# A hybrid two-layer trunk on one core: mixer boundaries in another order, and the first heads' side differences on GpSimd

## What is computed

```python
for layer in range(DEPTH):
    hn = rms_norm(x, norm_mix_pre[layer])
    if layer % 2 == 0:
        m = even_mixer(hn, even_w_in[i], even_gn[i], even_w_out[i], rel_bias, pos)   # RET + MoBA
    else:
        m = odd_mixer(hn, odd_w_in[i], odd_b_forget[i], odd_w_out[i])                # FoX
    x = x + rms_norm(m, norm_mix_post[layer])
    hn = rms_norm(x, norm_ffn_pre[layer])
    x = x + rms_norm(swiglu(hn, ffn_w_in[layer], ffn_w_out[layer]), norm_ffn_post[layer])
```

## Time and profile before

| | |
|---|---|
| three runs | 1187.09, 1187.13 and 1188.12 us, median 1187.13 us |
| profiled execution | 1187.56 us, of which the span from the first to the last instruction is 1185.5 us |
| TensorE busy | 1161.1 us, 98% of the span |
| VectorE, ScalarE, GpSimd busy | 712.2, 474.4 and 508.3 us |
| mean granted clock | 0.995 |

### The profile page before, as it was taken

One profiled execution on the slowest core, in us unless ns is written; L12 is line 12 of the kernel. 1 busy time (PEld: TensorE's weight loads), 2 busy tenths in 40 slices (PEclk: granted clock), 3 DMA queues, 4 the chain that ended last, 5 costly groups with the idle time before them and its releaser, 6 DMA issues.

```text
span 1185.5 us, 14108 instructions
## 1 busy us (share of the span) xinstructions
PE 1161.1 (98%) x5386; PEld 957.4 (81%) x5386; DVE 712.2 (60%) x939; ACT 474.4 (40%) x737; POOL 508.3 (43%) x282
## 2 busy tenths in 40 slices
PE   8999999979999999999999999999999999999998
PEld 6888886778888888888888888677988888888886
DVE  3786358464565566577455845876365546656673
ACT  5211347554233222175554333665523222225642
POOL 5745541676444454300467443009744445440004
PEclk9999999989999999999999999999999999999999
DMA  7899702626887332366664243025478843235663
GB/s 273 300 329 336 242 9 72 196 89 227 310 286 274 126 104 88 97 185 194 194 269 135 93 153 104 26 71 196 150 257 287 301 175 106 88 97 151 194 195 118
DMA packets 73460, 210.40 MB, mean 177 GB/s; under 512 B 5523, under 2 KB 5779, under 8 KB 73024
## 3 DMA queue, kind: packets, MB, share of 16 engines
q1 hardware_dynamic: 69496, 196.45, 49.7%
q10 hardware_dynamic: 3912, 13.27, 3.3%
HBM read 176.12 MB, written 34.89 MB: 178 GB/s over the span
## 4 chain that ended last, share of the span: by engine, by line
PE 73%; DVE 2%; ACT 1%; DMA 1%; issue 1%; POOL 1%; DVEq 0%; POOLq 0%; ACTq 0%
PE ps L1455 24%; PE ps L1457 24%; PE ps L1456 24%; DMA w_raw<-weights 1%; PE ps L1748 1%; PE ps L1713 1%; PE ps L1494 0%; POOL w_lo L442 0%; DVE x L976 0%; PE ps L1731 0%; DVE h_lo L997 0%; DVE ps L1112 0%; DVE work L1123 0%; DVE gate_x L991 0%; ACT h_hi L690 0%
## 5 line engine op out<-in xcount | busy, mean ns | idle before, releaser
L442 POOL TENSOR_TENSOR w_lo<-w_raw,w_hi 128x1024 fp32r<-128x1024 f32 (+1 forms) x191 | 463.3, 2437 | 624.7 <-ACT w_hi L567 623.0
L1455 PE MATMUL ps<-h_hi,w_hi 128*128 128x512 f32 (+1 forms) x1008 | 385.4, 382 | 7.5 <-DVE h_lo L997 7.5
L567 ACT ACTIVATE w_hi<-w_raw 128x1024 fp32r<-128x1024 f32 x252 | 257.1, 1032 | 328.1 <-DMA w_raw<-weights 210.5
L1457 PE MATMUL ps<-h_hi,w_lo 128*128 128x512 f32 (+1 forms) x1008 | 383.8, 381 | 0.0
L1456 PE MATMUL ps<-h_lo,w_hi 128*128 128x512 f32 (+1 forms) x1008 | 383.7, 381 | 0.0
L1455 PEld LDWEIGHTS ps<-h_hi,w_hi 128*128 128x128 f32 x1008 | 191.5, 190 | 43.7 <-DVE h_lo L997 8.0
L1456 PEld LDWEIGHTS ps<-h_lo,w_hi 128*128 128x128 f32 x1008 | 191.4, 190 | 35.7 <-issue 0.2
L1457 PEld LDWEIGHTS ps<-h_hi,w_lo 128*128 128x128 f32 x1008 | 191.4, 190 | 35.5
L1156 DVE TENSOR_TENSOR prod<-work,ps 128x512 f32<-128x512 f32 x44 | 30.3, 688 | 192.7 <-ACT work L755 192.7
L1457 PE MATMUL ps<-w_hi,prod_r 128*128 128x512 f32 x308 | 119.8, 389 | 0.0
L755 ACT ACTIVATE work<-ps 128x512 f32<-128x512 f32 x44 | 26.3, 598 | 219.7 <-PE ps L1457 219.7
(11 more groups left out here) (171 smaller groups left out, 1386.7 us busy)
## 6 DMA issues: line engine op xcount, KB each, us to landing
w_raw<-weights SPq DMA_DIRECT2D x140, 512.0 KB, 3.4
stage<-fold_w SPq DMA_DIRECT2D x22, 1024.0 KB, 8.3
fold_t<-stage SPq DMA_DIRECT2D x22, 1024.0 KB, 5.4
w_raw<-fold_t SPq DMA_DIRECT2D x40, 512.0 KB, 4.2
w_raw<-fold_w SPq DMA_DIRECT2D x30, 512.0 KB, 4.1
stage<-fold_o SPq DMA_DIRECT2D x8, 1024.0 KB, 8.0
fold_ot<-stage SPq DMA_DIRECT2D x8, 1024.0 KB, 5.2
w_raw<-fold_ot SPq DMA_DIRECT2D x16, 512.0 KB, 3.9
```

Of the source, the lines that this page charges most:

```text
L442: nc.gpsimd.tensor_tensor(w_lo[:, c % RING, 0:n], w_raw[:, c % RING, 0:n], w_hi[:, c % RING, 0:n].bitcast(F32), ALU.subtract).then_inc(lo_ ...
L567: nc.scalar.activation(w_hi[:, c % RING, 0:n], w_raw[:, c % RING, 0:n], ACT.Copy).then_inc(hi_done, 1)
L1455: mm(to, held[0], moved[0], start=start, stop=False, skip_group_check=more)
L1457: return mm(to, held[1], moved[0], start=False, stop=stop, skip_group_check=more)
```

## The change

Seven parts, all in the order of work; every sum is still formed.

1. The difference S3 of the heads in places 0 to 3 and its low part go from VectorE to GpSimd (`third_sides`), which reads the SBUF copies. In layer 0 this stands before `low(OUT0 + 3)`, in layer 1 before `low(OUT1 + 6)`. New semaphores carry it.
2. The high and low parts of the sides of places 4 and 5 get steps of their own in the attention tables; those of 6 and 7 stand at the start of `project_out`.
3. ScalarE makes the high parts of four output-weight chunks in layer 0 and two more in layer 1 within the attention steps.
4. TensorE does product 4 by rows, tile 0 of both chunks first, and VectorE merges and scales this tile at once; the rest of VectorE's boundary moves into `project_out` in a new order.
5. GpSimd's order in the boundaries 1 and 3.
6. ScalarE's order there.
7. `turn(b, 2)` moves from before the second half chunk to before the third.

The diff, cut to what the text speaks of (semaphores, the waits that change with them, the side operations of ScalarE and VectorE and VectorE's step tables are left out):

```diff
...
                 c0 = AFTER[b]
                 if b in (1, 3):
                     half_eps(b, 0, 2)
-                else:
-                    half_eps(b)
+                    post_rstds(b, 0)
+                    low(c0)
+                    post_rstds(b, 1)
+                    pre_rstds(b, 0)
+                    pre_rstds(b, 1)
+                    low(c0 + 1)
+                    half_eps(b, 2, 4)
+                    post_rstds(b, 2)
+                    post_rstds(b, 3)
+                    low(c0 + 2)
+                    pre_rstds(b, 2)
+                    pre_rstds(b, 3)
+                    low(c0 + 3)
+                    return
+                half_eps(b)
                 post_rstds(b, 0)
                 post_rstds(b, 1)
                 if b < 4:
                     low(c0)
                     pre_rstds(b, 0)
                     pre_rstds(b, 1)
-                    if b in (1, 3):
-                        half_eps(b, 2, 4)
                     low(c0 + 1)
                 for t in (2, 3):
                     post_rstds(b, t)
                     if b < 4:
                         low(c0 + t)
                         pre_rstds(b, t)
...
+
+            def third_sides(layer):
+
+                raw, side, held = head_raw[layer], side_raw[layer][S3_], side_r[layer][S3_]
+
+                def side_low(k):
+                    pool.wait_ge(third_hi, KH * layer + k + 1)
+                    nc.gpsimd.tensor_tensor(held[:, k, 1, :], side[:, k, 1, :], held[:, k, 0, :].bitcast(F32),
+                                            ALU.subtract).then_inc(third_ready, 1)
+                for k in range(KH):
+                    pool.wait_ge(raw_copied, KH * layer + k + 1)
+                    nc.gpsimd.tensor_tensor(side[:, k, 1, :], raw[:, k, 2 * P:SEQ], raw[:, k, 0:2 * P],
+                                            ALU.subtract).then_inc(third_summed, 1)
+                    if k:
+                        side_low(k - 1)
+                side_low(KH - 1)
 
             own(nc.gpsimd.memset(minus_half[:], -0.5))
             pre_rstds(0, 0)
@@ -537,13 +565,16 @@
                 y = ret_y_rows[:, h, :].rearrange("p (t d) -> p t d", d=HEAD)
                 pool.wait_ge(ret_normed, h + 1)
                 nc.gpsimd.tensor_tensor(y, y, ret_gate[:, :, h * HEAD:(h + 1) * HEAD], ALU.mult).then_inc(ret_y, 1)
+            third_sides(0)
             lows(OUT0 + 3, FIN0)
             boundary(1)
             lows(FIN0 + AHEAD, FOUT0)
             lows(FOUT0, FOUT0 + 6)
             lows(FOUT0 + 36, V1)
             boundary(2)
-            lows(V1 + AHEAD, FIN1)
+            lows(V1 + AHEAD, OUT1 + 6)
+            third_sides(1)
+            lows(OUT1 + 6, FIN1)
             boundary(3)
             lows(FIN1 + AHEAD, FOUT1)
             lows(FOUT1, FOUT1 + 6)
...
                 if b in (1, 2, 3):
                     c0 = AFTER[b]
                     sums(0, True, False)
+                    if b != 2:
+                        high(c0)
                     sums(1, True, False)
-                    high(c0)
+                    if b == 2:
+                        high(c0)
                     sums(0, False, True)
                     sums(1, False, True)
-                    if b in (1, 3):
-                        half_squares(b, (2, 3))
                     high(c0 + 1)
                     turned_high(b, 0)
-                    sums(2, True, False)
-                    high(c0 + 2)
-                    turned_high(b, 1)
-                    sums(2, False, True)
-                    sums(3, True, False)
-                    high(c0 + 3)
-                    sums(3, False, True)
+                    if b != 2:
+                        half_squares(b, (2, 3))
+                        turned_high(b, 1)
+                        sums(2, True, False)
+                        high(c0 + 2)
+                        sums(3, True, False)
+                        high(c0 + 3)
+                        sums(2, False, True)
+                        sums(3, False, True)
+                    else:
+                        sums(2, True, False)
+                        high(c0 + 2)
+                        turned_high(b, 1)
+                        sums(2, False, True)
+                        sums(3, True, False)
+                        high(c0 + 3)
+                        sums(3, False, True)
                     turned_high(b, 2)
                     turned_high(b, 3)
                     if b == 1:
...
                 5: lambda: head_high(RET_PLACE[1]), 6: lambda: copy_moba_v(3),
-                11: lambda: head_high(RET_PLACE[2]), 15: lambda: head_high(RET_PLACE[3]), 17: load_gains})
-            project_out(0, OUT0, OUT0 + 4)
+                11: lambda: head_high(RET_PLACE[2]), 15: lambda: head_high(RET_PLACE[3]), 17: load_gains,
+                8: lambda: high(OUT0 + 4), 13: lambda: high(OUT0 + 5), 18: lambda: high(OUT0 + 6), 20: lambda: high(OUT0 + 7),
+                16: lambda: side_highs(KH), 19: lambda: side_highs(KH + 1)})
+            project_out(0, OUT0, OUT0 + 8)
             boundary(1)
             ffn(0)
...
 
-            attention(FOX, TILES * MOBA, FOX_PLACE, FOX_BANKS, {5: lambda: high(OUT1 + 5)})
+            attention(FOX, TILES * MOBA, FOX_PLACE, FOX_BANKS, {
+                5: lambda: high(OUT1 + 5), 14: lambda: high(OUT1 + 6), 24: lambda: high(OUT1 + 7),
+                30: lambda: side_highs(KT + KH), 34: lambda: side_highs(KT + KH + 1)})
             act.dma_start(gain_pre[:], norms[3, 0].partition_broadcast(P)).then_inc(gain_pre_landed, 16)
...
                     vec.wait_ge(raw_copied, KH * (hd // KT) + hd % KT + 1)
                 nc.vector.tensor_tensor(h_lo[:, hd % KT, :], ps[:, 5 + 2 * (hd % 2), :],
                                         h_hi[:, hd % KT, :].bitcast(F32), ALU.subtract).then_inc(head_ready, 1)
-                head_sums(hd)
-                if hd % KT:
-                    side_lows(hd - 1)
+                if hd % KT >= KH:
+                    head_sums(hd)
 
             def head_sums(hd):
 
                 layer, place, k = hd // KT, hd % KT, hd % KH
                 bank, raw, n = ps[:, 5 + 2 * (hd % 2), :], head_raw[hd // KT], sums_of_heads(hd)
                 s3, s1, s2, s4 = (s[:, k, 1, :] for s in side_raw[layer])
-                if place < KH:
-                    nc.vector.tensor_tensor(s3, bank[:, 2 * P:SEQ], raw[:, k, 0:2 * P], ALU.subtract).then_inc(head_summed, 1)
-                    return
+                if place == KH:
+                    vec.wait_ge(raw_copied, KH * (layer + 1))
                 if hd == KH:
...
                     vec.wait_ge(merged, seen + 2 + t + 1)
                     merge(ps[:, 1 + 2 * t, :], 5 + 2 * t, work[:, 2 + t, :])
                 half_scale(b, (0, 1))
-                for t in range(2):
-                    vec.wait_ge(chunk_used, c0 + 10)
-                    merge(ps[:, 2 * t, :], 2 * t, work[:, t, :])
-                post(b, 0)
+                vec.wait_ge(first_row, layer + 1)
+                merge(ps[:, 0, :], 0, work[:, 0, :])
+                post_scale(b, 0)
+                vec.wait_ge(chunk_used, c0 + 10)
+                merge(ps[:, 2, :], 2, work[:, 1, :])
+                post_add(b, 0)
                 post(b, 1)
+                pre(b, 0)
                 for t in range(2):
                     vec.wait_ge(chunk_used, c0 + 12)
                     merge(ps[:, 5 + 2 * t, :], 5 + 2 * t, work[:, t, :])
+                pre(b, 1)
+                turned_low(b, 0)
+                half_scale(b, (2, 3))
+                turned_low(b, 1)
+                post(b, 2)
+                post(b, 3)
+                pre(b, 2)
+                pre(b, 3)
+                turned_low(b, 2)
+                turned_low(b, 3)
 
             def attention(heads, unit0, places, banks, table, also={}):
...
                 pe.wait_ge(h_ready, 4 * b + 2)
                 n = AHEAD - 1 if b else AHEAD
                 for i in range(n):
-                    if i == (1 if b else AHEAD - 1):
+                    if i == (n - 1 if b else AHEAD - 1):
                         turn(b, 2)
                     if i == n - 1:
...
@@ -1591,11 +1656,15 @@
                 product(1)
                 pe.wait_ge(probs, end)
                 product(2)
-                pe.wait_ge(head_summed, 16 * (layer + 1))
+                pe.wait_ge(head_summed, 3 * KH * (layer + 1))
                 pe.wait_ge(head_ready, KT * (layer + 1))
                 product(3)
                 pe.wait_ge(merged, seen + 4)
-                product(4)
+                for i in range(2):
+                    last = out_part(layer, 4, i, (0,))
+                last.then_inc(first_row, 1)
+                for i in range(2):
+                    out_part(layer, 4, i, (1,)).then_inc(chunk_used, 1)
                 pe.wait_ge(merged, seen + 6)
                 product(5)
                 pe.wait_ge(first_copied, 4 * layer + 2)
...
```

(23 more changed lines are left out.)

33 lines of the change are left out of this document (18 added, 15 removed).

## The result

Fourteen runs of the changed kernel gave 1192.59 us in the median (1187.1 to 1195.49), fourteen of the kernel before 1187.46 (1186.24 to 1188.56). The ratio is 1.004, 95% interval 1.0028 to 1.0052. The forecast was 1190.0 us. The profiled execution of the changed kernel took 1193.1 us, 5.5 more than that of before.

A forecast was written before the change was run, and what follows sets the result against it. TensorE, busy 98% of the span, was taken as the bound. From 1187.56 us, −0.5 and +3.75 (boundaries), −0.4 (FoX) and 0 (MoBA) gave 1190.4, or 1190.0 on the median; range 1180.5 to 1193.5.

The forecast's parts named there:

- Step 1: Both boundaries, first transposed tiles: they come about 0.7 us earlier, so TensorE's wait becomes 2.6 us.
- Step 3: Both boundaries, pre(2): GpSimd's low part ahead of rstd_pre(2) delays it; TensorE waits 0.4 to 0.6 us.
- Step 4: Both boundaries, pre(3): GpSimd's low part goes first and blocks it; turn(b, 3) waits 3.1 us, bounds 0.5 and 3.1.
- rival A: Boundaries, pre(3): VectorE goes first and the low part is stretched instead; 1181.4 us, chance 0.25.
- Step 5: Both boundaries, low clock after TensorE's waits: 0.5 us for the wait of 2.6, 1.9 for that of 3.1.
- FoX: FoX heads: VectorE's relief gives −2.3 us, a low part blocking s2 of head 4 costs 2.0; net −0.4, bounds −2.4, +1.5.
- rival B: Head stretches: the locks make a product wait 2 to 3 us and bring low clock; 1193.4 us, chance 0.17.
- MoBA: MoBA heads: VectorE's relief of 1.2 to 2 us against s2 blocked up to 2; taken as 0, bounds −2, +3.

The follow-up runs named there:

- the second experiment: Changed kernel, but GpSimd's low parts of output weights in the head stretches wait for VectorE's subtraction s2 of a head; 1193.04 us.
- the first experiment: Changed kernel, but in both boundaries GpSimd starts the fourth weight chunk's low part only after the last pre, pre(3); 1185.92 us.

## Why the prediction was right, and which terms were mis-sized

The side and the mechanism were right: slower, by the lock of the two engines at `pre(3)` and `s2`. Step by step:

- **Step 1** (first wait 2.6): 2.44 in both boundaries. Right.
- **Step 3** (`pre(2)` 5.0 us after TensorE's start): 838.00 − 833.02 = 4.98. Right. TensorE did not wait for it: it was at half clock and came later.
- **Step 4** (low part first, `pre(3)` done 10.5 us after the start): done at 843.37, 10.35 after. Right, and rival A is out: 0.12 us of lead were enough for GpSimd. The wait was 2.04 to 2.07, not 3.1, because the low clock had already delayed `turn(b, 2)`: in the second experiment, without a low clock ahead of it, it was 2.99 in both boundaries.
- **Step 5** (clock 0.5 and 1.9): one stretch of 3.4 us follows the first wait in either boundary, worth 1.7, and a second one the later wait in layer 1 alone. The mis-sized term: I gave the wait of 2.6 too little. Together 6.2 us in the first boundary (8.7 foreseen) and 7.9 in the second: −3.0 and +3.0 against −0.5 and +3.75.
- **FoX** (−0.4, at most +1.5): +3.7. This term failed. The lock was foreseen in place and length (2.42, 2.0 more), but only as idle time. With the 2.82 us of wait came 6.8 us of half clock, 5.95 / 2 = 3.0 lost, outside my bounds. Without the low clock, in the profile of the first experiment, the same stretch is 0.9 over the kernel before, inside them. It is close to rival B's mechanism, though what waited was a transpose of the softmax and not a product, and it belonged into the likeliest case.
- **MoBA** (0, bounds −2 and +3): +2.1, of which 1.7 are the clock stretch at 205.6. Within the bounds.

The errors are of both signs and partly cancel; the sum, +2.85, came out at +5.5 in the profiled execution. The median, 1192.59, lies nearer to rival B's 1193.4 than to the forecast of 1190.0, and near the upper end of the range (1180.5 to 1193.5). By the granted clocks of its runs, 0.996 in the fastest and 0.989 to 0.991 in the slowest, the low clock has a large part in where it lies, so the number is in part luck. The first boundary's gain was real, and so was the relief of VectorE: with the low parts out of the way the same change is 0.65% faster than the kernel before.

## What to carry to other kernels

Before work is given to GpSimd or started earlier, list VectorE's operations with two SBUF inputs on the critical chain and see which GpSimd operation starts just ahead of each: one of 2.4 us held such an operation up by 2.0 us here, and the same one placed behind it, 1.45 us later, cost nothing. Putting it directly behind such an operation can hand the collision to the next one, as at `s2`; look for a stretch in which VectorE reads PSUM. A meeting with slack behind it, as at `pre(1)`, costs nothing. When a TensorE wait is priced, the clock stretch that followed waits of its size in the trace belongs to the price, as a chance and not as a certainty.
